# Grouped-query attention on one Trainium2 core: who inverts the softmax row sums, and a new order of the trunk

## The chip, the cores and the metric

The kernel runs on one core of one Trainium2 chip. Its time is the device time of one execution in microseconds (us), and the figure compared is the median over runs. Five engines work side by side, each through a queue of its own in fixed order: TensorE (PE; its weight loads are listed as PEld), VectorE (DVE), ScalarE (ACT), GpSimd (POOL), and SyncE (SP), which issues the DMAs. An engine waits only where its program holds a wait on a semaphore.

## The reference

One encoder layer for two sequences of 1024 and 512 tokens, model width 1024, all float32. Every projection is computed with operands split into a high and a low part. The part that the change touches is the attention of the first block, and there the grouped-query heads:

```python
def _gqa_attention(q, k, v):
    scale = HEAD_DIM ** -0.5
    kf = k.astype(jnp.float32)

    def block(qb):
        s = jnp.einsum('bkgqd,bksd->bkgqs', qb.astype(jnp.float32), kf) * scale
        p = jax.nn.softmax(s, axis=-1)
        return jnp.einsum('bkgqs,bksd->bkgqd', p.astype(v.dtype), v)
...
x = x + jnp.einsum('bse,ed->bsd', jnp.concatenate([d_out, g_out], axis=-1), w_out)
```

d_out comes from four differential heads (two softmaxes, one subtracted from the other), g_out from eight grouped-query heads of width 64 in two groups. Behind the block follow cross-attention to 256 memory tokens, a feed-forward layer with a convolution of width 3, and the last norm.

## The kernel before

The trunk (`trunk_phase`) computes the input projection and all attention of the first block; the rest of the layer is a second program behind it. The trunk goes through six units: 0 to 3 are the differential heads, 4 and 5 the two grouped-query groups. While unit u's attention runs, the projection of unit u + 1 runs between it, 12 tiles of 128 tokens (index i = 12 u + t, so tiles 60 to 71 are unit 5's). Unit 5's attention has no projection beside it.

Attention is cut into 72 pairs. A pair is two tiles of 128 queries of one head against all keys of their sequence. Pairs 24 to 47 are unit 4's, 48 to 71 unit 5's; within a unit four heads of four pairs with 1024 keys come first (the long part), then four heads of two pairs with 512 keys (the short part). A grouped-query pair has two rows of scores (n, one for each query tile) and goes like this:

- PE `score`, DVE `max` (L1153, the negated row maximum), ACT `exp` (L1017, which sums the row as well, into `row_sum`),
- DVE `inverse` (L1158), the reciprocal of the row sum,
- POOL `scale` (L758), which multiplies the row by it in `prob`,
- PE `turn` (L896, four transposes of 128x128 for each 256 keys; the first one waits for both rows' `scale`), ACT `hi` (L1026), DVE `lo` (L1173), PE `mix` (L917), and at the end ACT `out` (L1043), DVE `merge` (L1192), SP `store`.

A tile of a grouped-query projection goes PE `proj` (L843), ACT `nat`, then POOL `v_split` (L698, L702), DVE `head_mean`, POOL `head_rstd` (L707), DVE `head_norm`, POOL `rope`, `turn_round` and `rope_add` (L731 to L752), PE `qk_turn` (L856), ACT `qk_hi`, DVE `qk_lo`. POOL also scales and splits the next unit's weights (`w_scale`, `w_split`: L672, L674) and, in unit 5, splits w_out in 16 steps (`out_split`: L681, L684). `rstd` (L657) is a power of one column.

The order on each engine isn't written by hand. `plan` puts every step with an engine, a due time, a duration and what it comes after; `Plan.placed` then fills the engines in turn. A step's rank is its due time plus a shift out of the table `SHIFT`, by stage (`dl`, `ds`: differential, long and short; `gl`, `gs`: grouped-query; `d`, `g`: projections) and by kind; `PATIENCE` says how long an engine's place is kept for an earlier step. The result is a fixed list of steps for each engine, and the semaphores alone decide when each runs.

## Time and profile before

| what | us |
|---|---|
| median of 3 runs | 2415.27 |
| lowest and highest | 2414.86, 2416.46 |
| the profiled execution | 2416.07 |
| its span, first to last instruction | 2414.3 |
| PE busy | 2356.2 (98%) |
| DVE busy | 1693.5 (70%) |
| POOL busy | 1399.2 (58%) |
| ACT busy | 1016.3 (42%) |

Busy shares are averages over stages that differ. The trunk ends at about 872 us; the rest belongs to the second program. In a row of a timeline the first number is the start in us from the span's start, the second the time to the end of the group, and a bracket at the end tells how long the engine had been idle and who ended that. Matmuls overlap one another, so a busy PE isn't a PE at its peak, and a short wait can hide in a matmul that only looks long.

### The profile page before, as it was taken

The numbers are of one execution on the slowest core, as the hardware profiler recorded it, in microseconds if no ns is written. First come the engines' busy times: TensorE is split into PE (matmuls) and PEld (weight loads), VectorE is DVE, ScalarE is ACT, GpSimd is POOL, SyncE is SP. The second block draws the span as 40 slices with busy tenths as digits, with TensorE's granted clock in tenths as the row PEclk, the third lists the DMA queues.
The fourth block names the chain that finished last, engine by engine and source line by source line (L and its number), as shares of the span: only waits on it lengthen the run. The fifth ranks groups of instructions, "written<-read, shape, count | busy, mean of one in ns | idle before, by whom it ended". The sixth has DMA issues, their size and how long they took to land.

```text
span 2414.3 us, 34261 instructions
## 1 busy us (share of the span) xinstructions
PE 2356.2 (98%) x12306; PEld 2017.4 (84%) x12306; DVE 1693.5 (70%) x2508; ACT 1016.3 (42%) x2047; POOL 1399.2 (58%) x1603
## 2 busy tenths in 40 slices
PE   7999999999999999999999999999999999999997
PEld 6999888888898878888888888888878888888885
DVE  7537777787889963243334388877688888888887
ACT  4436656555668852133332213211243333333334
POOL 5454645689877630053230277767777777777775
PEclk9999999999999999999999999999999999999999
DMA  8743434432212062132244323223321111111112
GB/s 297 248 173 139 158 136 159 159 131 98 96 61 85 13 193 106 45 121 72 100 152 141 138 98 105 92 92 105 140 83 62 53 53 53 53 53 53 53 53 92
DMA packets 102728, 260.40 MB, mean 108 GB/s; under 512 B 10145, under 2 KB 45345, under 8 KB 92065
## 3 DMA queue, kind: packets, MB, share of 16 engines
q1 hardware_dynamic: 101264, 257.82, 31.0%
q8 instruction: 100, 1.64, 0.3%
q14 instruction: 68, 0.55, 0.1%
q10 hardware_dynamic: 1296, 0.39, 0.1%
HBM read 209.95 MB, written 48.23 MB: 107 GB/s over the span
## 4 chain that ended last, share of the span: by engine, by line
PE 57%; DVE 2%; POOL 2%; ACT 1%; issue 1%; DMA 1%; DVEq 0%; POOLq 0%; SPq 0%; ACTq 0%
PE r_bank L2104 27%; PE r_bank L2010 11%; PE r_bank L1981 10%; PE r_bank L2043 5%; PE r_bank L2062 1%; PE r_bank L2091 1%; DVE r_conv L2474 1%; PE r_bank L2025 1%; PE r_bank L2074 0%; DMA r_rows_w<-in_w_up_units 0%; POOL r_s_lo L1849 0%; ACT r_conv L2311 0%; DVE r_x_p L2677 0%; DVE r_x_p L2552 0%; POOL r_w_lo L1849 0%
## 5 line engine op out<-in xcount | busy, mean ns | idle before, releaser
L843 PE MATMUL t_proj<-t_w_hi,t_hbuf 128*128 128x384 f32 x1056 | 311.6, 348 | 2.1 <-ACT t_nat L994 0.9
L2552 DVE TENSOR_TENSOR r_x_p<-r_bank,r_x_p 128x512 f32<-128x512 f32 x320 | 207.9, 683 | 47.1 <-PE r_bank L2104 46.5
L2474 DVE SCALAR_TENSOR_TENSOR r_conv<-r_rows,r_taps,r_conv 128x511 f32<-128x511 f32 (+3 forms) x134 | 182.5, 1362 | 49.4 <-ACT r_conv L2311 47.0
L1153 DVE TENSOR_REDUCE t_max_neg<-t_scores 128x1 f32<-128x1024 f32 (+1 forms) x192 | 196.9, 1038 | 23.8 <-PE t_scores L877 17.8
L1017 ACT ACTIVATE t_prob<-t_scores,t_max_neg 128x1024 f32<-128x1024 f32 (+1 forms) x192 | 187.4, 977 | 48.6 <-DVE t_max_neg L1153 44.5
L843 PEld LDWEIGHTS t_proj<-t_w_hi,t_hbuf 128*128 128x128 f32 x1056 | 194.9, 189 | 8.3 <-issue 6.4
L1026 ACT CAST t_pt_hi<-t_turn 128x512 fp32r<-128x512 f32 x240 | 140.3, 587 | 107.3 <-PE t_turn L896 82.2
L1173 DVE TENSOR_TENSOR t_pt_lo<-t_turn,t_pt_hi 128x512 fp32r<-128x512 f32 x240 | 163.4, 686 | 30.1 <-ACT t_pt_hi L1026 26.4
L843 PE MATMUL t_proj<-t_w_lo,t_hbuf 128*128 128x384 f32 x528 | 177.9, 337 | 0.0
L1776 POOL TENSOR_TENSOR r_stat<-r_stat,minus_half 128x1 f32<-128x1 f32 x24 | 14.1, 589 | 275.7 <-DVE r_stat L2437 275.7
L1831 POOL TENSOR_TENSOR r_w_lo<-r_stage,r_w_hi 128x1024 fp32r<-128x1024 f32 (+1 forms) x86 | 166.3, 1934 | 7.2
L896 PE MATMUL t_turn<-ident,t_prob 128*128 128x128 f32 x960 | 142.6, 274 | 6.2 <-DVE t_pt_lo L1173 4.2
L2278 ACT CAST r_s_hi<-r_s_raw 128x512 fp32r<-128x512 f32 x86 | 53.4, 620 | 219.8 <-POOL r_s_raw L1884 81.5
L917 PE MATMUL t_acc<-t_pt_hi,t_v_hi 128*128 128x256 f32 x480 | 139.0, 307 | 2.2 <-DVE t_pt_lo L1173 1.1
L1828 POOL TENSOR_SCALAR r_w_hi<-r_stage 128x1024 fp32r<-128x1024 f32 (+1 forms) x86 | 85.0, 988 | 93.5 <-PE r_bank L2104 48.7
L1981 PE MATMUL r_bank<-r_hs_hi,r_w_hi 128*128 128x512 f32 x352 | 137.1, 390 | 0.0
L1981 PE MATMUL r_bank<-r_hs_lo,r_w_hi 128*128 128x512 f32 x352 | 137.0, 389 | 0.0
L1981 PE MATMUL r_bank<-r_hs_hi,r_w_lo 128*128 128x512 f32 x352 | 136.9, 389 | 0.0
L2486 DVE TENSOR_TENSOR r_x_s<-r_bank,r_x_s 128x512 f32<-128x512 f32 x176 | 120.3, 688 | 23.0 <-PE r_bank L2104 21.3
L1849 POOL TENSOR_TENSOR r_s_lo<-r_s_raw,r_s_hi 128x512 fp32r<-128x512 f32 x86 | 115.5, 1343 | 35.1 <-ACT r_s_hi L2278 35.1
L2104 PE MATMUL r_bank<-r_wd_hi,r_g_hi 128*128 128x512 f32 x336 | 131.1, 390 | 1.9 <-DVE r_g_lo L2547 1.4
L896 PEld LDWEIGHTS t_turn<-ident,t_prob 128*128 128x128 f32 x960 | 111.8, 140 | 24.3 <-issue 11.6
(307 smaller groups left out, 7282.9 us busy)
## 6 DMA issues: line engine op xcount, KB each, us to landing
t_hbuf<-split_x SPq DMA_DIRECT2D x60, 1024.0 KB, 4.8
r_stage<-in_w_up_units SPq DMA_DIRECT2D x44, 512.0 KB, 3.3
r_rows_w<-in_w_up_units SPq DMA_DIRECT2D x88, 256.0 KB, 3.1
split_x<-t_hbuf SPq DMA_DIRECT2D x12, 1024.0 KB, 5.2
r_stage<-in_w_down SPq DMA_DIRECT2D x22, 512.0 KB, 3.3
r_wd_raw<-in_w_down SPq DMA_DIRECT2D x42, 256.0 KB, 2.7
...
```

The source lines that it names most:

```text
L843: ins = nc.tensor.matmul(proj_bank(i), l, r[:, k, :], start=(k == 0 and j == 0), stop=(k == KT - 1 and j == 2))
L896: ins = nc.tensor.transpose(ps_t[:, slot, kk * 2 * P + qt * P:kk * 2 * P + (qt + 1) * P], prob[:, n % PSLOTS, keys], ident[:, :])
L1017: nc.scalar.activation(prob[:, n % PSLOTS, 0:p.keys], ps_s[:, n % 2, 0:p.keys], ACT.Exp, bias=max_neg[:, n % COLS:n % COLS + 1], accum_out ...
L1026: nc.scalar.copy(pt_hi[:, n % 2, :], ps_t[:, slot, :]).then_inc(pthi_done, 1)
L1153: nc.vector.tensor_reduce(max_neg[:, n % COLS:n % COLS + 1], ps_s[:, n % 2, 0:p.keys], AX.X, ALU.max, negate=True).then_inc(max_done, 1)
L1173: nc.vector.tensor_tensor(pt_lo[:, n % 2, :], ps_t[:, slot, :], f32(pt_hi[:, n % 2, :]), ALU.subtract).then_inc(ptlo_done, 1)
L1831: nc.gpsimd.tensor_tensor(lo, raw, f32(hi), ALU.subtract).then_inc(w_split[s], 1)
L1981: ins = nc.tensor.matmul(one_bank(s), l, r, start=(k == 0 and j == 0), stop=(k == KT - 1 and j == 2))
L2010: ins = nc.tensor.matmul(acc(t)[:, cols], l[:, k, :], r[:, cols], start=(k == 0 and j == 0), stop=(k == KT - 1 and j == 2))
L2104: ins = nc.tensor.matmul(out, l, r, start=(first and j == 0), stop=(last and j == 2), skip_group_check=onto)
L2474: return nc.vector.scalar_tensor_tensor(out, src, tap_of(j, s, i), out, ALU.mult, ALU.add)
L2552: nc.vector.tensor_tensor(x_p[:, t, cols], down_bank(n), x_p[:, t, cols], ALU.add).then_inc(p_add, 1)
```

## The change

The DVE `inverse` of the grouped-query pairs is gone (96 reciprocals; the differential pairs keep their 48). POOL waits for `exp` itself, raises the row sum to the power -1 against a column of -1.0, waits for its own result, and scales as before. In the plan the two steps become one of POOL with 0.55 more time. A rope of a differential tile now waits for the rope before it. `SHIFT` and `PATIENCE` have new values, so that steps of every stage stand in other places.

```diff
-PATIENCE = {"PE": 0.03, "DVE": 0.23, "ACT": 0.36, "POOL": 0.23, "SP": 0.0}
+PATIENCE = {"PE": 0.03, "DVE": 0.26, "ACT": 0.34, "POOL": 0.19, "SP": 0.0}
 SHIFT = {
...
-    "gl": {"exp": -5.7, "hi": -3.5, "inverse": -0.7, "lo": -21.9, "max": -3.2, "merge": -28.7, "mix": 1, "out": -2.2, "scale": 0.3,
+    "gl": {"exp": 3.8, "hi": -3, "inverse": -0.7, "lo": -20.7, "max": -1.3, "merge": -26.7, "mix": 1.4, "out": -2.5, "scale": 0.6,
...
-                put("DVE", b + 3.8 * s, 0.17, "inverse", (p, n), ("exp", (p, n, 0)))
-                put("POOL", b + 4.1 * s, by_seg(1.13, 0.71), "scale", (p, n), ("inverse", (p, n)))
+                put("POOL", b + 3.8 * s, by_seg(1.68, 1.26), "scale", (p, n), ("exp", (p, n, 0)))
...
+            nc.gpsimd.memset(minus_one[:, :], -1.0).then_inc(minus_made, 1)
...
                     if UNITS[u][0] == "diff":
                         pool.wait_ge(nat_filled, i + 1)
+                        if i:
+                            pool.wait_ge(roped, i)
...
                 elif kind == "scale":
                     p, n = what
-                    pool.wait_ge(inv_done, n - 2 * n_diff + 1)
+                    pool.wait_ge(exp_done, n + 1)
+                    if n == 4 * n_diff:
+                        pool.wait_ge(minus_made, 1)
+                    nc.gpsimd.tensor_tensor(inv[:, n % COLS:n % COLS + 1], row_sum[:, n % COLS:n % COLS + 1], minus_one[:, 0:1],
+                                            ALU.pow).then_inc(row_inverted, 1)
+                    pool.wait_ge(row_inverted, n - 4 * n_diff + 1)
```

What the new order looks like at three places follows, of the kernel before and of the changed one. Line numbers of the changed kernel are higher by 1 to 8: L762 is the new power, L766 the scaling, L682 and L685 the two instructions of a split of w_out.

POOL in the long part of unit 5, before, from the scalings of pair 52 to those of pair 53 (`wo_hi`, `wo_lo` are the parts of w_out):

```order
L758 TENSOR_SCALAR t_prob<-t_prob,t_inv 128x1024 x2
L681 TENSOR_SCALAR wo_hi_73<-wo_raw_89 128x512
L684 TENSOR_TENSOR wo_lo_81<-wo_raw_89,wo_hi_73 128x512
L681 TENSOR_SCALAR wo_hi_73<-wo_raw_89 128x512
L684 TENSOR_TENSOR wo_lo_81<-wo_raw_89,wo_hi_73 128x512
L758 TENSOR_SCALAR t_prob<-t_prob,t_inv 128x1024 x2
```

and in the changed kernel, from the second row of pair 52:

```order
L762 TENSOR_TENSOR t_inv<-t_row_sum,t_minus_one 128x1
L766 TENSOR_SCALAR t_prob<-t_prob,t_inv 128x1024
L682 TENSOR_SCALAR wo_hi_73<-wo_raw_89 128x512
L685 TENSOR_TENSOR wo_lo_81<-wo_raw_89,wo_hi_73 128x512
L762 TENSOR_TENSOR t_inv<-t_row_sum,t_minus_one 128x1
L766 TENSOR_SCALAR t_prob<-t_prob,t_inv 128x1024
L682 TENSOR_SCALAR wo_hi_73<-wo_raw_89 128x512
L685 TENSOR_TENSOR wo_lo_81<-wo_raw_89,wo_hi_73 128x512
L762 TENSOR_TENSOR t_inv<-t_row_sum,t_minus_one 128x1
```

Two splits between two pairs have become, mostly, one split between two rows, and they reach on to pair 61 instead of pair 57; each scaling has its power in front.

POOL at the end of unit 4, before, the last tile (71) and pairs 45 to 50 (L731, L739, L744, L750, L752 are its rope):

```order
L707 TENSOR_TENSOR t_vrstd<-t_vstat,minus_half 128x5
L758 TENSOR_SCALAR t_prob<-t_prob,t_inv 128x512 x2
L731 TENSOR_TENSOR t_nat<-t_nat,t_head_gain 128x320
L739 TENSOR_TENSOR t_rot_a<-t_nat,t_cos_g 128x320
L744 TENSOR_TENSOR t_rot_b<-t_nat,t_sin_g 128x5x16 x4
L758 TENSOR_SCALAR t_prob<-t_prob,t_inv 128x512 x2
L750 TENSOR_TENSOR t_nat<-t_rot_a,t_rot_b 128x256
L752 TENSOR_TENSOR t_nat<-t_rot_a,t_rot_b 128x128
L758 TENSOR_SCALAR t_prob<-t_prob,t_inv 128x512
L758 TENSOR_SCALAR t_prob<-t_prob,t_inv 128x1024 x5
```

and in the changed kernel, from the same rope on:

```order
L734 TENSOR_TENSOR t_nat<-t_nat,t_head_gain 128x320
L762 TENSOR_TENSOR t_inv<-t_row_sum,t_minus_one 128x1
L766 TENSOR_SCALAR t_prob<-t_prob,t_inv 128x512
L742 TENSOR_TENSOR t_rot_a<-t_nat,t_cos_g 128x320
L747 TENSOR_TENSOR t_rot_b<-t_nat,t_sin_g 128x5x16 x4
L753 TENSOR_TENSOR t_nat<-t_rot_a,t_rot_b 128x256
L755 TENSOR_TENSOR t_nat<-t_rot_a,t_rot_b 128x128
L762 TENSOR_TENSOR t_inv<-t_row_sum,t_minus_one 128x1
L766 TENSOR_SCALAR t_prob<-t_prob,t_inv 128x512
L762 TENSOR_TENSOR t_inv<-t_row_sum,t_minus_one 128x1
L766 TENSOR_SCALAR t_prob<-t_prob,t_inv 128x1024
```

Pair 47's first scaling has moved ahead of the long turn of tile 71's rope; its second still stands behind the rope's end.

PE at the same place, before: the first transposes of pair 47 (L896), the eight matmuls of pair 46's mix (L917), then tile 71's qk_turn (L856) and the scores of pair 49's second row:

```order
L896 MATMUL t_turn<-ident,t_prob 128x128 x4
L917 MATMUL t_acc<-t_pt_hi,t_v_hi 128x256
...
L917 MATMUL t_acc<-t_pt_lo,t_v_hi 128x256
L856 MATMUL t_turn<-ident,t_nat 128x128 x3
L882 MATMUL t_scores<-t_qk_109 128x512
```

and in the changed kernel:

```order
L864 MATMUL t_turn<-ident,t_nat 128x128 x3
L925 MATMUL t_acc<-t_pt_hi,t_v_hi 128x256
...
L925 MATMUL t_acc<-t_pt_lo,t_v_hi 128x256
L904 MATMUL t_turn<-ident,t_prob 128x128 x4
L890 MATMUL t_scores<-t_qk_109 128x512
```

Tile 71's qk_turn and pair 47's first transposes have changed places around the mix of pair 46.

## Rows read from the trace of the kernel before

**Rows 1.** Busy time by stretch: window, length, then each engine's busy time (instructions).
```profile
150.00:573.00 423.00, 416.91 (x2574) 370.83 (x2573) 310.36 (x587) 242.72 (x635) 260.29 (x552) 1.00 0.42 149
583.10:748.50 165.40, 161.13 (x1083) 148.95 (x1083) 144.73 (x282) 117.33 (x255) 133.76 (x208) 1.00 0.20 68
756.00:837.00 81.00, 80.70 (x579) 73.41 (x578) 78.50 (x136) 71.61 (x133) 64.53 (x64) 1.00 0.22 65
837.00:872.00 35.00, 29.91 (x202) 24.37 (x201) 29.13 (x61) 27.70 (x62) 9.70 (x14) 1.00 0.20 50
```
The engines stand in the order PE, PEld, DVE, ACT, POOL; behind them the granted clock, the DMA share and GB/s.

**Rows 2.** Timeline of DVE in unit 5: start, duration, engine, line, operation.
```profile
814.69 0.15 DVE L1158 RECIPROCAL t_inv<-t_row_sum 128x1 f32<-128x1 f32 x1
814.76 1.21 DVE L1153 TENSOR_REDUCE t_max_neg<-t_scores 128x1 f32<-128x1024 f32 x1
```

**Rows 3.** Line L758: POOL's idle time before it; who waited for it (us, times).
```profile
  DVE t_inv L1158: 49.4, 35
...
  PEld t_turn L896: 4.8, 9
```

**Rows 4.** Timeline of PE: the first transposes of pairs 58, 59 and 62.
```profile
811.82 0.60 PE L896 MATMUL t_turn<-ident,t_prob 128*128 128x128 f32 x4
...
817.32 0.38 PE L896 MATMUL t_turn<-ident,t_prob 128*128 128x128 f32 x2
...
833.55 0.60 PE L896 MATMUL t_turn<-ident,t_prob 128*128 128x128 f32 x4
```

**Rows 5.** Timeline of POOL at the start: a power of one column and its reader.
```profile
31.78 0.56 POOL L657 TENSOR_TENSOR t_rstd<-t_mean_sq,minus_half 128x1 f32<-128x1 f32 x1
32.44 1.19 POOL L661 TENSOR_SCALAR t_mem_diag<-ident,t_rstd 128x128 f32<-128x128 f32 x1
```

**Rows 6.** Timeline of POOL: the scalings of pairs 58 and 59 in one go.
```profile
809.33 4.43 POOL L758 TENSOR_SCALAR t_prob<-t_prob,t_inv 128x1024 f32<-128x1024 f32 x4
```

**Rows 7.** Timeline of POOL: the starts of two splits of w_out that follow each other.
```profile
761.22 0.63 POOL L681 TENSOR_SCALAR wo_hi<-wo_raw 128x512 fp32r<-128x512 f32 x1
...
763.19 0.62 POOL L681 TENSOR_SCALAR wo_hi<-wo_raw 128x512 fp32r<-128x512 f32 x1
```

**Rows 8.** Timeline of ACT: the end of pair 50's first exp, its row sum read out.
```profile
758.23 0.20 ACT L1017 ACTIVATION_READ_ACCUMULATOR t_prob<-t_scores,t_max_neg 128x1 f32 x1
```

**Rows 9.** Timeline of POOL: unit 4's first scalings and its last one.
```profile
583.08 2.25 POOL L758 TENSOR_SCALAR t_prob<-t_prob,t_inv 128x1024 f32<-128x1024 f32 x2
...
747.75 0.69 POOL L758 TENSOR_SCALAR t_prob<-t_prob,t_inv 128x512 f32<-128x512 f32 x1 [0.32 <-DVE t_inv L1158]
```

**Rows 10.** POOL's waits from 583 to 748 us: total, times, longest.
```profile
POOL t_prob L758 <- DVE t_inv L1158: 11.7, 10, 2.8
POOL t_nat L731 <- DVE t_nat L1128: 6.8, 8, 1.6
POOL t_v_hi L698 <- ACT t_nat L994: 5.7, 3, 3.0
POOL t_vrstd L707 <- DVE t_vstat L1122: 4.2, 10, 1.1
```

**Rows 11.** Timeline of POOL: scalings of pairs 48 to 50, first and last of five.
```profile
750.49 1.13 POOL L758 TENSOR_SCALAR t_prob<-t_prob,t_inv 128x1024 f32<-128x1024 f32 x1 [2.05 <-DVE t_inv L1158]
...
760.13 1.13 POOL L758 TENSOR_SCALAR t_prob<-t_prob,t_inv 128x1024 f32<-128x1024 f32 x1 [0.66 <-DVE t_inv L1158]
```

**Rows 12.** Timeline of PE: the first transposes of pair 47.
```profile
749.60 0.60 PE L896 MATMUL t_turn<-ident,t_prob 128*128 128x128 f32 x4
```

**Rows 13.** PE's waits from 500 to 872 us on VectorE's lo: total, times, longest.
```profile
PE t_turn L896 <- DVE t_pt_lo L1173: 4.2, 5, 1.3
...
PE t_acc L917 <- DVE t_pt_lo L1173: 1.1, 2, 0.6
```

**Rows 14.** Timeline of POOL and of PE: pair 38's scalings, then its first transposes.
```profile
693.30 2.40 POOL L758 TENSOR_SCALAR t_prob<-t_prob,t_inv 128x1024 f32<-128x1024 f32 x2 [0.50 <-DVE t_inv L1158]
...
707.81 0.60 PE L896 MATMUL t_turn<-ident,t_prob 128*128 128x128 f32 x4
```

More of the change, by code:

```diff
@@ L131 @@
 RING = {"turn": "lo", "qk_turn": "qk_lo", "sumsq": "sub_mean", "spread": "finish", "total": "mean"}
-PATIENCE = {"PE": 0.03, "DVE": 0.23, "ACT": 0.36, "POOL": 0.23, "SP": 0.0}
+PATIENCE = {"PE": 0.03, "DVE": 0.26, "ACT": 0.34, "POOL": 0.19, "SP": 0.0}
 SHIFT = {
-    "dl": {"coef": -20.2, "combine": 6, "eps_r": 29.7, "exp": 3.9, "finish": 8.6, "hi": 7.7, "inverse": -50.1, "lo": 9, "max":
-          19.8, "mix": 5.2, "out": 11.2, "score": 1.3, "spread": -12.7, "store": 5.4, "sub_mean": 2, "sub_rstd": 11, "sumsq":
-          -72.3, "turn": -0.5},
-    "ds": {"coef": -18.7, "combine": -16.4, "eps_r": -16.7, "exp": -3.3, "finish": -31.2, "hi": -6.7, "inverse": 43.7, "lo": 8.4,
-          "max": -15.7, "mix": 5.1, "out": 7.2, "score": -5.6, "spread": -0.8, "store": 0.8, "sub_mean": 21.1, "sub_rstd": -38.7,
-          "sumsq": -22.8, "turn": 1.8},
-    "gl": {"exp": -5.7, "hi": -3.5, "inverse": -0.7, "lo": -21.9, "max": -3.2, "merge": -28.7, "mix": 1, "out": -2.2, "scale": 0.3,
-          "score": -1.7, "store": 28.5, "turn": 0.4},
-    "gs": {"exp": -4.8, "hi": -4, "inverse": -1.6, "lo": -1.4, "max": -4.5, "merge": -0.6, "mix": -36.7, "out": -2.9, "scale":
-          -0.6, "score": -0.2, "store": -13.7, "turn": 2.5},
-    "g": {"head_mean": -7.2, "head_norm": -8.8, "head_rstd": 16.7, "nat": -2.6, "proj": 0.1, "qk_hi": -42.5, "qk_lo": 15.5,
-         "qk_turn": 0.2, "rope_add": 1.6, "rope": 8, "turn_round": -15.5, "v_split": 16.5},
-    "d": {"nat": -42.3, "proj": -2.8, "qk_hi": 47.1, "qk_lo": 19.3, "qk_turn": 0.2, "rope": 5.3, "v_split": 9.7},
@@ new lines @@
+    "dl": {"coef": -41.7, "combine": 4.1, "eps_r": 25.8, "exp": 6.9, "finish": 18.6, "hi": 15.6, "inverse": -36.8, "lo": 6, "max":
+          9.7, "mix": 6.8, "out": 10.9, "score": 1.3, "spread": 1.6, "store": -22.4, "sub_mean": -28.3, "sub_rstd": -1.1, "sumsq":
+          -76.3, "turn": -0.6},
+    "ds": {"coef": -20.1, "combine": -9.2, "eps_r": -31.7, "exp": 5.7, "finish": -24.6, "hi": -4.7, "inverse": 71.7, "lo": -0.1,
+          "max": -19.8, "mix": 1.8, "out": 6, "score": -4.7, "spread": 0.9, "store": 1.6, "sub_mean": 41.4, "sub_rstd": -60.2,
+          "sumsq": -35.5, "turn": 1.8},
@@ new lines @@
+    "gl": {"exp": 3.8, "hi": -3, "inverse": -0.7, "lo": -20.7, "max": -1.3, "merge": -26.7, "mix": 1.4, "out": -2.5, "scale": 0.6,
+          "score": -1.2, "store": 50.5, "turn": 0.7},
+    "gs": {"exp": -4.5, "hi": -3.6, "inverse": -1.6, "lo": -1.8, "max": -3.6, "merge": -0.3, "mix": -41.4, "out": -3.2, "scale":
+          -9.9, "score": -0.2, "store": 10.9, "turn": 0.7},
+    "g": {"head_mean": -5.4, "head_norm": -11.3, "head_rstd": 17.2, "nat": -1.3, "proj": 0.5, "qk_hi": -37.2, "qk_lo": 20.9,
+         "qk_turn": 0.2, "rope_add": -20.7, "rope": 1.5, "turn_round": 4.7, "v_split": 16.5},
@@ L149 @@
+    "d": {"nat": -34.5, "proj": -2.8, "qk_hi": 53.3, "qk_lo": 10.2, "qk_turn": 0.7, "rope": 7, "v_split": 9.5},
 }
```

3 lines of the change are left out of this document (2 added, 1 removed).

## The prediction

> **What bounds the kernel now.** I read the busy table by stretch first. TensorE (PE) is busy 416.9 of 423.0 us in the differential units, 161.1 of 165.4 in the first grouped-query unit (unit 4, whose pairs are 24 to 47), 80.7 of 81.0 in the long part of unit 5 and 29.9 of 35.0 in its short part and drain [rows 1]. So PE sets the pace, and all that a better order can take back in the trunk is its idle time: 6.1 + 4.3 + 0.3 + 5.1 us, about 16. From 872 us on nothing is changed. In the same rows GpSimd (POOL) is at 133.8 of 165.4 in unit 4 and at 64.5 of 81.0 in unit 5; VectorE (DVE) is at 144.7 and 78.5. The question is whether Pool can take 96 more instructions before it overtakes PE.
>
> **The reciprocal that goes.** One lasts 0.15 us, but on VectorE's queue the next instruction starts 0.07 us after it (814.69 to 814.76) [rows 2]: 96 x 0.07 = 6.7 us of VectorE's time, up to 96 x 0.15 = 14.4 if none overlapped. Its wait also goes: Pool stood 49.4 us before its scalings for VectorE's inverse, which had queued behind lo and max steps [rows 3]. In the steady part of unit 5, pair 58 opens its transposes at 811.82 and pair 59 at 817.32, a period of 5.50 us [rows 4]; PE has no gap in it, so a lighter VectorE gives nothing there. I cost the removal at nothing. PE covers it; what would make it count is rival A.
>
> **The power that comes.** The kernel has a power of one column on Pool already, for rstd, and it is followed once, as the new one always is, by a wait of Pool on itself. It starts at 31.78, lasts 0.56, and the instruction that reads its result starts at 32.44 [rows 5]: 0.66 us from start to start. The bounds are 0.55, if the wait were free, and 0.66. I take 0.655, since every dependent pair on Pool shows the gap. A long scaling takes 1.10 (four in 4.43 us) [rows 6], so a long row now costs Pool 1.755 us. The whole addition is 96 x 0.655 = 63 us of Pool.
>
> **Unit 5: Pool against PE.** Between the scalings Pool splits w_out, 16 times 1.97 us (761.22 to 763.19) [rows 7]. Before, Pool did two splits and two scalings per pair, 6.15 us against PE's 5.50, for eight pairs, and used up its lead: pair 58's scalings began at 809.33, two of them end near 811.5, and its transposes opened at 811.82 [rows 4, 6]. The new order spreads the splits (first order piece). Sum from pair 50, whose first exp is read out at 758.43 [rows 8]: up to the scaling of pair 62 there are 26 rows x 1.755 = 45.6, plus 16 x 1.97 = 31.5, together 77.1, hence 835.6. PE opened pair 62's transposes at 833.55 [rows 4]. So Pool is 2.1 us late there even if it starts pair 50 on time. With 0.55 for the power it would be 74.4 and on time.
>
> **Unit 4: does Pool start pair 50 on time?** From its first scaling at 583.08 to the end of its last at 748.44 Pool has 165.4 us [rows 9]. Its waits for others in that stretch are 11.7 + 6.8 + 5.7 + 4.2 = 28.4 [rows 10], so its own chain takes 137.0. Add 48 x 0.655 = 31.4: 168.4, already 3 us more than there is, with no wait left. Some waits can't go: head_rstd is made on Pool, head_norm on VectorE, rope on Pool again. These were 6.8 us over 8 waits, 0.85 each [rows 10]. In the new order four of the fourteen tiles (58 to 71) still have rope right behind head_rstd, and three have only the short v_split between: 4 x 0.85 and some 0.2 for each of the three, together 4.0. So the last scaling of pair 47 ends near 755.5. Four scalings of pairs 48 and 49 (7.0) bring pair 50 to 762.5, 4.0 us later than its exp allows. Before, Pool had slack here: it waited 2.05 + 0.98 + 1.90 + 1.59 + 0.66 = 7.2 us before the five scalings from 750.49 to 760.13 (the first and the last of the five in [rows 11]), and this is what the new work eats. The lower end is 168.4 with no wait, which brings pair 50 back to 758.5 and the lateness to 2.1 alone. The upper end keeps all 11.0 us of waits on the head chain, which adds 7 more.
>
> In this stretch qk_turn and the first transposes of pair 47 change places on PE, and the last scaling of pair 47 stands behind rope_add on Pool (second and third order piece). PE opened pair 47 at 749.60, 1.16 us behind the scaling [rows 9, 12]. This is where I expect the first PE wait. Queued behind it are the scores of pair 49 and everything later.
>
> **The new order elsewhere.** The table moves steps in every unit. In the differential units Pool's work is unchanged but for a wait of each rope on the one before it, which has long ended; PE's idle time is 6.1 us in 423 [rows 1]. A new order could win or lose some 2 us of this; I take zero. SP's stores move by a place or two; the out_loads now stand ahead of pair 47's store, which delays nothing that is short. The drain at the end keeps its order: most of PE's waits for VectorE's lo are there, the longest 1.3 us [rows 13], and reciprocals stood ahead of it. There, and in the rest of unit 5's short part (5.1 us idle), I take 1 us back, since VectorE catches up while PE is late.
>
> **Sum.** 2.1 (unit 5) + 4.0 (unit 4) - 1 (drain) = +5.1, taken as +5. The profiled execution took 2416.07 with a span of 2414.3, so 1.8 us lie around the span; the median of the three runs is 2415.27, 0.8 below it. On the profiled one that gives 2421.1, against the median 2420.3.
>
> **A rule against this.** VectorE is the busiest of the three elementwise engines in unit 5, 97% against Pool's 80% [rows 1]. The Trainium skill, Perfetto Trace Analysis, Identifying the Most-Contended Engine, says that for Vector, Scalar and GPSIMD the occupancy tells how close an engine is to its limit, and to optimize the busiest engine first. By that rule the change moves load the right way, and the sum would be rival A's, not mine. The rows speak against it as far as they go: an average of 80% hides that Pool runs without a pause for eight pairs.
>
> **Rivals.**
> A. VectorE is the real pace-setter beside PE, and the change is faster. Mechanism: lo steps come 0.07 to 0.15 us earlier and never sit behind an inverse that waits for exp, so PE's waits on them go. From 500 to 872 us those are 4.2 + 1.1 = 5.3 us [rows 13]; nearly all of it, with a little of the rest of PE's idle time, is 5.5, giving 2409.8. It decides if Pool's lead never falls to zero. Against it: nine weight loads of transposes waited 4.8 us for Pool [rows 3], so Pool had little to give already. Chance 0.15.
> B. Pool's lag stays inside its lead. In the middle of unit 4 that is long: pair 38's second scaling ends at 695.70 and its transposes open at 707.81 [rows 14]. The new order also puts most of unit 4's qk_turn steps later. If Pool's waits vanish and scalings are ordered well, only small changes are left: -1.5 us, 2413.8, within 2 us either way. Chance 0.27.
> C. Pool holds PE up as summed: 2420.3, from +1 to +11. Chance 0.45. This is the forecast.
> D. The order of the differential units turns out worse: exp, combine and lo change places there too, and if a transpose comes to wait in each of the 24 pairs for 0.25 us, PE's idle time of 6.1 us [rows 1] doubles: 2421.3. Nothing in the profile speaks for it but the many moved steps. Chance 0.13.
>
> **How the numbers follow.** About 0.2%, 4.8 us, is what a measurement of this kernel can tell from no change. C straddles that bound: two thirds of it above (0.30), one third within (0.15). B is within but for 0.05. A is faster but for 0.03. D is slower but for 0.03. That makes faster 0.14, same 0.43, slower 0.43. The range leaves out A's better half and C's and D's worst ends: 2410.5 to 2427.
>
> **What would show it.** If C holds, Pool has hardly any idle time from 583 to 830 us, and the list of PE's waits has transposes waiting for t_prob from Pool, the first near pair 47 and qk_turn 71, again between pairs 53 and 62. The power followed by the scaling shows 0.65 us from start to start, and the span from 583 to 837 us grows while 872 to the end stays at 1542. If A holds, that stretch shrinks and VectorE shows gaps. If B holds, Pool is near 98% busy in unit 4 and PE doesn't wait for it. If D holds, the stretch up to 573 us grows. I am wrong at the root if the power costs under 0.5 us, or if the splits of w_out are far shorter than 1.97 between two powers.

## The result and the profile after

The changed kernel takes 2421.84 us (median of 10 runs, 2419.12 to 2424.03) against 2415.61 for the kernel before (10 runs, 2414.86 to 2416.46): a ratio of 1.0024, 95% interval 1.0016 to 1.0033, 6.2 us slower. The forecast was 2420.3, slower by 5. The number was nearly right. The profile shows another cause than the one that made it. The profiled execution of the changed kernel took 2424.03 with a span of 2421.9, so it is the longest of the ten.

First the stretches, as in [rows 1] (window, length, busy time of PE, PEld, DVE, ACT and POOL with instructions, granted clock, DMA share, GB/s):

```profile
150.00:573.00 423.00, 416.84 (x2575) 370.73 (x2574) 309.89 (x589) 242.73 (x632) 259.64 (x555) 1.00 0.42 150
583.00:749.00 166.00, 162.37 (x1094) 150.10 (x1093) 141.19 (x241) 118.92 (x258) 154.97 (x251) 1.00 0.20 68
756.00:837.00 81.00, 76.52 (x531) 70.31 (x530) 71.10 (x93) 66.18 (x122) 73.47 (x85) 0.96 0.20 64
```

Up to 573 us the busy times are those of before. In unit 4 POOL is up by some 21 us and PE is as busy as before. In the long part of unit 5 PE is at 76.52 of 81.0 where it had 80.70, and the granted clock is 0.96: the loss is there. PE's waits from 583 to 837 us (who waited for what: us in total, times, longest):

```profile
PE t_acc L925 <- DVE t_mixed L1200: 4.4, 1, 4.4
...
PE t_turn L904 <- POOL t_prob L766: 0.6, 1, 0.6
...
```

All but the first lie in unit 4 and at its end and come to 4.3 us; before, PE's waits in the same 254 us were 4.9, of which 0.9 for POOL. POOL, the engine of the forecast, costs PE one wait of 0.6 us (pair 48). The large one is a wait of `mix` (L925) for VectorE's merge, and the merge had waited for a DMA. The timelines of DVE and then of PE there (start, duration, and in brackets the idle time before with its releaser):

```profile
774.87 0.42 DVE L1200 TENSOR_TENSOR t_mixed<-t_acc,t_sq 64x256 f32<-64x256 f32 x1 [4.76 <-DMA mix_scratch<-t_mixed]
```

```profile
775.43 0.55 PE L925 MATMUL t_acc<-t_pt_hi,t_v_hi 128*128 128x256 f32 x1 [4.40 <-DVE t_mixed L1200]
776.00 0.41 PE L925 MATMUL t_acc<-t_pt_hi,t_v_hi 128*128 128x256 f32 x1
...
777.28 1.05 PE L904 MATMUL t_turn<-ident,t_prob 128*128 128x128 f32 x4
...
781.84 0.60 PE L904 MATMUL t_turn<-ident,t_prob 128*128 128x128 f32 x4
```

DVE stood 4.76 us before the merge of pair 49, which writes the same half of `mixed` as pair 47 and must wait until pair 47's store has landed. PE stood 4.40 us before the mix of pair 50, which waits for that merge. After the wait a matmul of the mix lasts 0.41 us and four transposes 1.05, until at 781.84 four transposes take their usual 0.60 again. In the windows around it the granted clock is the last but two number:

```profile
770.00:775.00 5.00, 1.03 (x7) 0.66 (x5) 0.24 (x2) 1.50 (x3) 4.71 (x7) 0.93 0.73 229
775.00:780.00 5.00, 4.57 (x17) 4.21 (x18) 3.40 (x5) 2.21 (x4) 4.47 (x5) 0.50 0.06 15
780.00:785.00 5.00, 5.00 (x38) 4.78 (x36) 4.03 (x5) 3.32 (x7) 4.11 (x6) 0.88 0.06 13
```

PE hardly ran until 775, and came back with a clock of 0.50, the lower of its two levels (1.2 of 2.4 GHz), from 775 to 780.

SP's queue shows why the store was late. After, and then before (`x8` is a group of eight; the second number is the time to the group's end):

```profile
756.91 13.89 SPq L633 DMA_DIRECT2D wo_raw<-in_w_out  x8
770.84 29.34 SPq L624 DMA_DIRECT2D mix_scratch<-t_mixed  x7
```

```profile
756.34 3.99 SPq L633 DMA_DIRECT2D wo_raw<-in_w_out  x3
760.38 0.45 SPq L624 DMA_DIRECT2D mix_scratch<-t_mixed  x1
761.29 9.62 SPq L633 DMA_DIRECT2D wo_raw<-in_w_out  x5
```

The store of pair 47 is the single one at 760.38 before. In the changed kernel it is the first of the seven at 770.84, behind all eight out_loads of 512 KB each, which SP issues some 1.74 us apart. It lands 4.0 us after its issue, while the loads are moving 229 GB/s; the store behind it takes 3.7, and those issued once the loads have ended take 1.9. Before, the same store took 4.4 us, also among loads, so it is late by its issue, 770.84 in place of 760.38, and not by its transfer. The Trainium skill, DMA: Bandwidth & Descriptors, Latency and other measured facts, says that a DMA's fixed cost grows with the load on HBM, which is where this store goes; the 4.0 against 1.9 us fits that, but would fit as well a store that only queues behind the loads' data, and no run here tells the two apart.

How late each pair is shows where time goes. The table has the opening of a pair's transposes against the kernel before, with the lateness at pair 0 taken off (it varies from -0.8 to +0.9 us between executions), from each kernel's profiled execution. "Minus before" is median against the median of before on the same chip.

| kernel | median us | minus before | at pair 50 | pair 50 to 62 | pair 62 to 71 |
|---|---|---|---|---|---|
| changed kernel | 2421.84 | +6.2 | +0.3 | +7.0 | 0.0 |
| x1 changed, store ahead of out_load 3 | 2417.62 | +1.4 | +0.2 | +1.9 | 0.0 |
| x2 before, store behind out_load 7 | 2423.99 | +7.7 | +0.7 | +7.5 | 0.0 |
| x3 power, order of before | 2434.75 | +18.5 | +8.9 | +9.7 | 0.0 |
| x4 new order, reciprocals, no power | 2425.11 | +8.8 | +6.2 | +0.1 | +3.1 |
| x5 changed, store behind out_load 5 | 2417.33 | +0.9 | -0.2 | +1.8 | 0.0 |
| x6 changed, store behind out_load 6 | 2420.09 | +3.6 | -0.3 | +4.8 | 0.0 |
| x7 as x1, reciprocals as well | 2421.46 | +5.0 | +1.9 | +1.7 | +3.3 |
| x8 as x3, reciprocals as well | 2432.39 | +15.9 | +7.9 | +9.5 | 0.0 |
| x9 as x1, splits spread | 2416.58 | +0.2 | +0.1 | +0.3 | 0.0 |
| x10 before with the new table, store ahead | 2424.10 | +7.7 | +7.6 | -0.1 | +0.5 |
| x11 as x3, splits spread | 2425.51 | +9.1 | +8.9 | +4.1 | 0.0 |
| x12 as x9, drain moved | 2415.32 | -1.7 | +0.1 | +0.8 | -1.8 |

### The profile page after: what moved, and what is told of

Its sections match the earlier page's. It is cut to its first block, busy times and chain, and to the rows that moved or that the text cites. A ratio compares the mean times of both kernels' runs of the same rounds, so it can differ in the third digit from the quotient of the medians.

```text
span 2421.9 us, 34310 instructions
## 1 busy us (share of the span) xinstructions
PE 2358.8 (97%) x12306; PEld 2019.2 (83%) x12306; DVE 1683.4 (70%) x2412; ACT 1016.8 (42%) x2047; POOL 1447.2 (60%) x1700
## 4 chain that ended last, share of the span: by engine, by line
PE 57%; DVE 2%; POOL 2%; ACT 1%; issue 1%; DMA 1%; DVEq 0%; POOLq 0%; SPq 0%; ACTq 0%
PE r_bank L2112 27%; PE r_bank L2018 11%; PE r_bank L1989 10%; PE r_bank L2051 5%; PE r_bank L2070 1%; PE r_bank L2099 1%; DVE r_conv L2482 1%; PE r_bank L2033 1%; PE r_bank L2082 0%; DMA r_rows_w<-in_w_up_units 0%; POOL r_s_lo L1857 0%; ACT r_conv L2319 0%; DVE r_x_p L2685 0%; DVE r_x_p L2560 0%; POOL r_w_lo L1857 0%
## 5 line engine op out<-in xcount | busy, mean ns | idle before, releaser
L1839 POOL TENSOR_TENSOR r_w_lo<-r_stage,r_w_hi 128x1024 fp32r<-128x1024 f32 (+1 forms) x86 | 166.3, 1934 | 7.2
L925 PE MATMUL t_acc<-t_pt_hi,t_v_hi 128*128 128x256 f32 x480 | 139.8, 308 | 7.4 <-DVE t_mixed L1200 5.4
```

Of the source, the lines that this page charges most:

```text
L1839: nc.gpsimd.tensor_tensor(lo, raw, f32(hi), ALU.subtract).then_inc(w_split[s], 1)
```

## The store

The first theory: all of the loss is the store's place on SP. The rival: Pool is late as forecast, and the stall only hides it.

**x1, the store back in its old place.**

```diff
     order = plan(pairs, bounds)
+    sp = order["SP"]
+    late = next(s for s in sp if s[1] == "store" and s[2][0].no == 47)
+    sp.remove(late)
+    sp.insert(next(z for z, s in enumerate(sp) if s[1:] == ("out_load", (3,))) + 0, late)
```

> The changed kernel, with one step of SyncE's queue moved: the store of pair 47 stands ahead of out_load 3, where the kernel before has it, in place of behind out_load 7. Nothing on any other engine moves. The theory of the store: in the changed kernel pair 51 opens its transposes 7.7 us later than before, and from there the lateness stays at 7.6 to 7.7 to the end of the trunk; all of it is the 4.8 us that VectorE waited for this store's transfer, passed on to TensorE (4.4), and what TensorE lost after it. So this kernel loses all of that: pair 51 within 1 us of the kernel before, 2414 to 2416 us, 6 to 8 below the changed kernel. The theory of the prediction, Pool as the bound: with the stall gone Pool's lateness comes out, TensorE waits for t_prob at pairs 53 to 62, 2.1 us by the prediction's sum for unit 5, so 2417 to 2418; with its whole sum of 5, 2420.

Measured: 2417.62 (2416.90 to 2418.79), 1.0005 of before (0.9996 to 1.0014). Of the 6.2 us above before 1.4 are left. The jump of 7.0 between pairs 50 and 51 is gone; pairs 51 and 50 are both 0.25 us earlier than before. But the time is not back at before's: 1.9 us are lost between pairs 50 and 62. PE's waits from 755 to 837 us in this kernel:

```profile
PE t_turn L908 <- POOL t_prob L770: 1.8, 2, 1.4
```

These are pair 53 (0.37) and pair 58 (1.39), and there is no other wait in the stretch. So both theories hold in part: the store made the loss of the changed kernel, and behind its stall lay the lateness of Pool, 1.9 us where the prediction's sum has 2.1.

**x2, the same fault put into the kernel before.** Here only the store moves, behind out_load 7.

```diff
     order = plan(pairs, bounds)
+    sp = order["SP"]
+    late = next(s for s in sp if s[1] == "store" and s[2][0].no == 47)
+    sp.remove(late)
+    sp.insert(next(z for z, s in enumerate(sp) if s[1:] == ("out_load", (7,))) + 1, late)
```

> The kernel before (reciprocals on VectorE, its own order), with one step moved: the store of pair 47 stands behind out_load 7, as in the changed kernel, in place of ahead of out_load 3. The theory of the store: the merge of pair 49 waits some 4 to 5 us for the transfer, TensorE's mix of pair 50 waits with it, and what follows is at the low clock for a few us: 6 to 8 us slower than before, 2421 to 2424, with the jump between pairs 50 and 51 and nothing else changed. The rival, that the store only hurts together with Pool's new load (Pool being the bound): within 1 us of before, since Pool here has its old work.

Measured: 2423.99 (2423.24 to 2424.96), 7.7 above before. The wait and its releaser are the same as in the changed kernel:

```profile
775.36 0.55 PE L921 MATMUL t_acc<-t_pt_hi,t_v_hi 128*128 128x256 f32 x1 [5.13 <-DVE t_mixed L1196]
```

One DMA issue of 64 KB, moved on a queue where nothing computes, costs 7.7 us without any change to Pool or VectorE. The rival falls.

**x5 and x6, the store one and two places earlier than the change has it.** The edit is x1's, with `("out_load", (5,))` or `("out_load", (6,))` and `+ 1`.

> The changed kernel with the store of pair 47 behind out_load 5, two places earlier than the change has it. The out_loads are issued some 1.74 us apart (eight from 756.91 to 770.84), so the store lands 3.5 us earlier and TensorE's wait for the mixed tile of pair 50 should be 4.4 - 3.5 = 0.9 us in place of 4.4. In the changed kernel pair 51 is 7.0 us later against pair 50, of which 4.4 are the wait and 2.6 the low clock behind it. If the clock falls after any such wait, the jump is 0.9 + 2.6 = 3.5 and the time near 2421; if a wait this short leaves the clock alone, the jump is 0.9 and the time stays within 1 us of the kernel with the store ahead of out_load 3 (2417.6), since Pool's lateness of 1.9 up to pair 62 hides under those 0.9 partly.

> The changed kernel with the store of pair 47 behind out_load 6, one place earlier than the change has it: the wait should be 4.4 - 1.7 = 2.7 us. If what follows the wait is the low clock at the same price as in the changed kernel, the jump from pair 50 to pair 51 is 2.7 + 2.6 = 5.3 and the time near 2421; if the price grows with the wait, less than 2.6 is added; if the clock stays up, the jump is 2.7 and the time is near 2418.5, Pool's lateness of unit 5 then being hidden behind it.

Measured: 2417.33 (2416.36 to 2419.15) and 2420.09 (2417.95 to 2423.01). The stalls of PE in them, in that order:

```profile
770.22 0.36 PE L929 MATMUL t_acc<-t_pt_hi,t_v_hi 128*128 128x256 f32 x1 [0.25 <-DVE t_mixed L1204]
```

```profile
774.13 0.55 PE L929 MATMUL t_acc<-t_pt_hi,t_v_hi 128*128 128x256 f32 x1 [3.54 <-DVE t_mixed L1204]
```

and the window behind x6's stall:

```profile
775.00:780.00 5.00, 5.00 (x31) 4.76 (x31) 3.46 (x5) 3.11 (x6) 4.72 (x7) 0.76 0.06 15
```

Put together, with the lateness gained from pair 50 to pair 53:

| kernel | PE's wait for `mixed`, us | lateness gained | beyond the wait |
|---|---|---|---|
| x5 | 0.25 | 0.29 | 0.0 |
| x12 | 0.78 | 0.80 | 0.0 |
| x11 | 2.55 | 4.11 | 1.6 |
| x6 | 3.54 | 5.01 | 1.5 |
| changed | 4.40 | 6.97 | 2.6 |
| x2 | 5.13 | 7.52 | 2.4 |

A wait of 0.25 us, or one of 0.78 (x12, which gains 0.80), leaves the clock at 1.00 in every window. Behind one of 3.54 it is 0.76 from 775 to 780, behind one of 4.40 it is 0.50. The price of the clock was 1.5 to 1.6 us in two kernels and 2.4 to 2.6 in two, so of the cases in the two expectations the one of a short wait that leaves the clock alone (x5) and the one of a price that isn't constant (x6) came true. The waits themselves missed: 0.25 for 0.9, and 3.54 for 2.7. SP doesn't issue the out_loads evenly, 1.74 us is only their mean: in the changed kernel out_load 5 goes out at 765.67 and out_load 6 at 768.85. So x5's store went out 5.5 us earlier (765.37) and not 3.5, and x6's 1.6 earlier (769.20), with a landing of 4.3 us in place of 4.0 and a PE that had come to the mix 0.45 us earlier.

## Pool, and the power against the reciprocal

**x3, the power alone.** The changed kernel's code with the table and the planner's lines of before; the `inverse` of a grouped-query pair is skipped on VectorE.

```diff
-PATIENCE = {"PE": 0.03, "DVE": 0.26, "ACT": 0.34, "POOL": 0.19, "SP": 0.0}
+PATIENCE = {"PE": 0.03, "DVE": 0.23, "ACT": 0.36, "POOL": 0.23, "SP": 0.0}
...
-                put("POOL", b + 3.8 * s, by_seg(1.68, 1.26), "scale", (p, n), ("exp", (p, n, 0)))
+                put("DVE", b + 3.8 * s, 0.17, "inverse", (p, n), ("exp", (p, n, 0)))
+                put("POOL", b + 4.1 * s, by_seg(1.13, 0.71), "scale", (p, n), ("inverse", (p, n)))
...
                 elif kind == "inverse":
                     p, n = what
+                    if not p.diff:
+                        continue
```

> The power alone: Pool inverts the row sums, VectorE's reciprocals of the grouped-query units are gone, and all engines keep the order of the kernel before (its table of numbers), the store ahead of out_load 3 included. By the arithmetic of Pool: in the first eight pairs of unit 5 it has two splits of 1.97 and two rows of 1.755 per pair, 7.45 us against TensorE's 5.50, 1.3 us per pair more than before, where its lead was just used up by pair 58; so some 10 us late at pair 58, and in unit 4 its own chain of 137.0 + 31.4 us against 165.4 with 11 us of waits on the head chain that the old order has, up to 7 us more. That gives 2425 to 2432, with many waits of TensorE for t_prob. The theory that Pool has room enough in any order: within 1.5 us of before, 2414 to 2417, and then the new order was needed for nothing and only did harm by the store.

Measured: 2434.75 (2434.08 to 2435.36), 18.5 above before, 2.8 more than the upper end of what I expected. Of the 8.9 us up to pair 50, 0.7 are lost in the differential units, at 465 us, where PE waits 1.2 us for a `lo` in place of 0.4; the only step that is new there is the wait of each rope on the one before it, and no run here takes that apart. Five pairs in a row, 54 to 58, each lose another 1.9 us. PE's waits in the long part of unit 5, and Pool's timeline over one pair:

```profile
PE t_turn L905 <- POOL t_prob L767: 9.7, 8, 1.7
```

```profile
797.97 0.55 POOL L763 TENSOR_TENSOR t_inv<-t_row_sum,t_minus_one 128x1 f32<-128x1 f32 x1
798.63 1.13 POOL L767 TENSOR_SCALAR t_prob<-t_prob,t_inv 128x1024 f32<-128x1024 f32 x1
799.72 0.55 POOL L763 TENSOR_TENSOR t_inv<-t_row_sum,t_minus_one 128x1 f32<-128x1 f32 x1
...
801.46 0.62 POOL L683 TENSOR_SCALAR wo_hi<-wo_raw 128x512 fp32r<-128x512 f32 x1
802.16 1.29 POOL L686 TENSOR_TENSOR wo_lo<-wo_raw,wo_hi 128x512 fp32r<-128x512 f32 x1
...
805.38 0.55 POOL L763 TENSOR_TENSOR t_inv<-t_row_sum,t_minus_one 128x1 f32<-128x1 f32 x1
```

From 797.97 to 805.38 Pool does two powers, two scalings and two splits without a pause, 7.41 us; PE's pair takes 5.50. The prediction's arithmetic gives 2 x 1.755 + 2 x 1.97 = 7.45. The power starts 0.66 us ahead of the scaling, and the scaling 1.09 ahead of the next step.

**x11, the power with the splits alone placed anew.** x3 with these lines; x9 is x1 with them.

```diff
+    pool = order["POOL"]
+    splits = [s for s in pool if s[1] == "out_split"]
+    pool[:] = [s for s in pool if s[1] != "out_split"]
+    for k, s in enumerate(splits):
+        pool.insert(next(z for z, x in enumerate(pool) if x[1] == "scale" and x[2][1] == pairs[50 + k].score + 1) + 1, s)
```

> The power in the order of before (2434.75), and of the new order only one thing: the 16 splits of w_out spread to one behind the second scaling of each pair from 50 to 65. In the run without that, pair 58 opened 9.6 us later against pair 53 than before, 1.9 us in each of five pairs, which is Pool's 7.45 us per pair against 5.50. By the same arithmetic with one split (5.48 against 5.50) nothing of it is left: 2425. The 8.9 us lost up to pair 50 stay, since unit 4 is as it was. If it falls by much less, the loss of unit 5 was not the splits.

Measured: 2425.51 (2423.82 to 2429.11), the 2425 of the expectation. From pair 53 to pair 62 nothing is lost any more, where x3 lost 9.6. The profiled execution is the slowest of the five: a merge in it waited 2.90 us for the store of pair 48, which took 6.3 us to land, so the late stores are still there. The 8.9 us up to pair 50 stay, as expected.

**x9, the changed kernel with the store ahead and the splits spread.** (The changed kernel has its 16 splits at pairs 50 to 61, most pairs with one; "two per pair" in the expectation is wrong.)

> The changed kernel with the store of pair 47 ahead of out_load 3 (2417.6), and Pool's 16 splits of w_out placed anew: one behind the second scaling of each pair from 50 to 65, in place of two per pair from 50 to 61. By Pool's arithmetic a pair then costs it 2 x 1.755 + 1.97 = 5.48 us, TensorE's period is 5.50, and what is left falls to pairs 63 to 65, where the scalings had 2 to 5 us to spare. In the kernel with the store ahead, pair 62 is 1.9 us later against pair 50 than before, with waits of 0.37 and 1.39 for t_prob. If Pool's splits make that, it goes: 2415.7. If another engine is late behind it (VectorE's lo, ScalarE's exp), the waits change their name and the time stays within 0.5 us of 2417.6.

Measured: 2416.58 (2415.63 to 2418.73), 1.0001 of before (0.9992 to 1.0010). The loss from pair 50 to 62 falls from 1.9 to 0.3, and PE's list for the long part of unit 5 has one row left:

```profile
PE t_acc L934 <- DVE t_mixed L1209: 0.2, 1, 0.2
```

So the change has two faults of order, one hidden behind the other, and with both mended it is as fast as the kernel before, not faster.

**Is the reciprocal worth nothing on VectorE?** Two kernels keep the power and put the 96 reciprocals back beside it, into a tile that nobody reads: x7 on x1's order, x8 on x3's. x4 is x7 without the power, its scaling waiting for the reciprocal as before.

```diff
+    dve = order["DVE"]
+    for p in pairs:
+        if p.diff:
+            continue
+        for n in (p.score, p.score + 1):
+            step = (0.0, "inverse", (p, n))
+            at = next((z for z, s in enumerate(dve) if s[1] == "max" and s[2][1] == n + 2), None)
+            if at is None:
+                at = next(z for z, s in enumerate(dve) if s[1:] == ("lo", (pairs[69], n - 190)))
+            at = min(at, next(z for z, s in enumerate(dve) if s[1] == "max" and s[2][1] == n) + 6)
+            dve.insert(at, step)
```

> The new order alone: the changed kernel's order on every engine, with the store of pair 47 ahead of out_load 3 as in the experiment above, but the reciprocals back on VectorE (each about two steps of max behind its own row), Pool without the power. Beside the kernel with the store ahead, this is the power against the reciprocal and nothing else. If Pool is the bound in it: 2 to 5 us faster than that one. If neither Pool nor VectorE sets the pace: within 1 us of it. If VectorE's lightened queue is what the change is worth (rival A): up to 5.3 us slower than it, the waits of TensorE for lo growing by as much.

> The kernel with the store ahead of out_load 3 (changed order, power on Pool, 2417.6), with VectorE's 96 reciprocals put back beside it, at the places that they had in the run of the order alone (2425.1); their result goes to a tile that nobody reads. So power and reciprocals both run. Rival A, that the reciprocals' place in VectorE's queue costs TensorE time in this order: the whole 7.5 us between those two runs are theirs, and this kernel is at 2424 to 2426. The theory of the prediction, that VectorE has room and the removal is worth nothing: within 1 us of 2417.6, and the 7.5 us of the run of the order alone came from Pool's scalings starting later, behind an inverse that VectorE makes late. In that run TensorE's waits between 640 and 740 us were for t_qk (1.8), t_pt_lo (1.7) and t_mixed (1.1), all written by VectorE, which speaks for the former.

> The run of the power in the order of before (2434.75), with VectorE's 96 reciprocals also left where the kernel before has them, their result going to a tile that nobody reads. Power and reciprocals both run; the difference to that run is what the removal alone gave in the old order, the difference to before is what the power alone costs. The prediction costed the removal at nothing: within 1 us of 2434.75. Rival A: slower than that by up to 5.3 us. VectorE is freed of 6.7 to 14.4 us, so if all of it told, it would be 2441 to 2449.

Measured: x4 2425.11 (2424.95 to 2426.27), x7 2421.46 (2420.55 to 2424.13), x8 2432.39 (2432.27 to 2434.05).

| | reciprocals only | both | power only |
|---|---|---|---|
| order of before | 2416.3 (before) | 2432.4 (x8) | 2434.8 (x3) |
| new order, store ahead | 2425.1 (x4) | 2421.5 (x7) | 2417.6 (x1) |

In the old order the removal of the reciprocals gains nothing; with them the kernel is even 2.4 us faster. 1.2 of that is in the trunk, the rest before pair 0, and I have no cause for it. In the new order x1 is 3.8 us faster than x7, and x7 3.6 faster than x4. What each difference is made of shows in the traces. First x7 against x1, whose profiled executions are 4.9 us apart at pair 71 (the medians 3.8). By the table of lateness 1.7 us arise up to pair 50 and 3.3 behind pair 62. The 3.3 begin at one place, DVE's and then PE's timeline in x7:

```profile
843.66 0.17 DVE L1182 RECIPROCAL t_spare<-t_row_sum 128x1 f32<-128x1 f32 x1 [1.96 <-ACT t_prob L1040]
843.74 1.27 DVE L1197 TENSOR_TENSOR t_pt_lo<-t_turn,t_pt_hi 128x512 fp32r<-128x512 f32 x2
```

```profile
844.47 0.38 PE L940 MATMUL t_acc<-t_pt_hi,t_v_hi 128*128 128x256 f32 x1 [2.14 <-DVE t_pt_lo L1197]
```

My rule put the reciprocal of pair 65's first row ahead of the last two lo of pair 62. It waited 1.96 us for exp, the two lo stood behind it, PE stood 2.14 us, and the granted clock from 845 to 850 was 0.66. x4 has the same place and loses 3.1 there. The planner's own places (x10, below) have that reciprocal behind the two lo, and the loss is 0.5. So the larger part of the difference is a place of my own choosing, and what the reciprocals cost in this order otherwise is the 1.7 us up to pair 50 or a little less. No run moves that one step alone.

Then x4 against x7, which have the same list of steps on every engine and differ in Pool's scaling: in x7 it has the power ahead of it and waits for exp, in x4 it waits for VectorE's reciprocal. From 583 to 756 us, in x4:

```profile
POOL t_prob L776 <- DVE t_inv L1176: 27.3, 21, 3.9
```

In x7 it never does. x4 is 6.2 us late at pair 50, x7 1.9. PE's waits for VectorE from 640 to 740 us, in x4,

```profile
PE t_turn L914 <- DVE t_qk L1166: 1.8, 1, 1.8
PE t_turn L874 <- DVE t_pt_lo L1191: 1.5, 1, 1.5
PE t_acc L935 <- DVE t_mixed L1210: 1.1, 1, 1.1
PE t_acc L935 <- DVE t_pt_lo L1191: 0.2, 1, 0.2
```

and in x7:

```profile
PE t_acc L940 <- DVE t_mixed L1216: 1.1, 1, 1.1
...
PE t_turn L879 <- DVE t_pt_lo L1197: 0.3, 1, 0.3
PE t_acc L940 <- DVE t_pt_lo L1197: 0.2, 1, 0.2
```

They come to 4.6 and 1.6 us; in x1 it is 0.5. VectorE's name stands on all of x4's, but 3.0 of the 4.6 go with the same reciprocals still on VectorE, as soon as Pool no longer waits for them. Whether other places for the reciprocals would save the loss up to pair 50 is what x10 tests.

**x10, the new table alone,** in the kernel before, with x1's store.

> The kernel before with nothing but the changed table of numbers, the reciprocals on VectorE and put in their places by the planner itself (a median of seven steps behind their row's max, like before), and the store of pair 47 ahead of out_load 3. In the run of the order alone the reciprocals stood at places of my own choosing, one to six steps behind the max. If their places made the loss there (2425.1), this kernel is well below it, 2416 to 2418. If the new numbers need a VectorE without reciprocals, it stays at 2421 or more, with TensorE's waits for t_qk, t_pt_lo and t_mixed between 640 and 740 us.

Measured: 2424.10 (2423.28 to 2425.29), 1.0 us below x4. The planner's own places take away the loss behind pair 62 (0.5 for 3.1) but not the one up to pair 50 (7.6). So the new numbers need the reciprocals off VectorE's path to Pool. By x4 against x7 (6.2 and 1.9 us at pair 50) Pool's wait for them is the larger part of that and their time on VectorE the smaller; for the planner's own places no run takes the two apart. Each half of the change alone costs time (18.5 and 7.7 us); together, with the store mended, they cost 1.4. The comparison is of the tables, not of one order, since 237 of the 1113 places in PE's list hold another step when the planner has reciprocals to place.

**x12, the drain.** In nearly all these kernels PE waits for VectorE's lo at pairs 70 and 71. In x9, DVE and then PE there:

```profile
861.67 1.22 DVE L1214 TENSOR_TENSOR h_lo<-h_raw,h_hi 128x1024 fp32r<-128x1024 f32 x1
862.80 0.69 DVE L1190 TENSOR_TENSOR t_pt_lo<-t_turn,t_pt_hi 128x512 fp32r<-128x512 f32 x1
```

```profile
863.64 0.63 PE L913 MATMUL t_turn<-ident,t_prob 128*128 128x128 f32 x4 [1.24 <-DVE t_pt_lo L1190]
...
867.21 0.63 PE L913 MATMUL t_turn<-ident,t_prob 128*128 128x128 f32 x4 [1.05 <-DVE t_pt_lo L1190]
```

A step of 1.22 us (`mix_lo`, L1214) stands right ahead of a lo, and at 865.19 another, of 1.28; in the kernel before, a reciprocal between them took 0.07. x12 moves those two, and the two casts of ACT that they wait for.

```diff
+    act, dve = order["ACT"], order["DVE"]
+    for queue, kind, behind in ((act, "mix_hi", [("hi", (pairs[70], 1)), ("hi", (pairs[71], 1))]),
+                                (dve, "mix_lo", [("lo", (pairs[70], 1)), ("lo", (pairs[71], 1))])):
+        for t, at in enumerate(behind):
+            step = next(s for s in queue if s[1:] == (kind, (t,)))
+            queue.remove(step)
+            queue.insert(next(z for z, s in enumerate(queue) if s[1:] == at) + 1, step)
```

> The kernel with the store ahead and the splits spread (2416.6), and in the drain four steps moved: ScalarE's mix_hi of tiles 0 and 1 behind hi of pair 70 and of pair 71, VectorE's mix_lo of the same tiles behind lo of pair 70 and of pair 71. In that kernel, and in every other one here, TensorE waits 1.24 and 1.04 us for lo at pairs 70 and 71. The prediction said that reciprocals stood ahead of those lo steps and took 1 us back with them; without reciprocals the waits are the same. Theory: it is the mix_lo steps of 1.22 and 1.28 us, which stand right ahead of lo on VectorE. Moved, the waits go, up to the 1.8 us that Pool's scaling of pair 71 has to spare, less some 0.3 at the end where mix_lo now delays the last merge: 2415.1, 1.5 below that kernel and 1.3 below the kernel before. If the lo steps are late for another reason (hi, exp), the waits stay and so does the time.

Measured: 2415.32 (2414.16 to 2417.16), 0.9995 of before (0.9986 to 1.0004), so not told apart from it. PE's timeline:

```profile
864.14 0.63 PE L920 MATMUL t_turn<-ident,t_prob 128*128 128x128 f32 x4 [0.41 <-DVE t_pt_lo L1197]
...
870.84 0.36 PE L941 MATMUL t_acc<-t_pt_hi,t_v_hi 128*128 128x256 f32 x1 [1.31 <-DVE t_mixed L1216]
...
874.41 0.76 PE L2034 MATMUL r_bank<-wo_hi,h_hi 128*128 128x512 f32 x1 [2.32 <-PEq L454]
```

The wait at pair 70 falls from 1.24 to 0.41 and the one at pair 71 is gone; pair 71 opens 1.8 us earlier against pair 62. But the last mix now waits 1.31 us for a merge that stands behind a moved `mix_lo`, and the second program's first matmul comes at 874.41. From the opening of pair 62 to that matmul it is 39.35 us, against 40.13 in x9: 0.8 us gained. (Counted from pair 0 only 0.26 is left of it, since this execution lost 0.5 us more at pair 51, whose mix waited 0.78 us for a merge in place of 0.21.) The medians of x12 and x9 are 1.3 us apart, from two chips and with intervals that overlap, so they don't tell 0.8 from the 1.5 that I expected. The cause was right; by the traces about half of the gain came, since the wait moved on by one pair.

## The prediction, step by step

- **The power, 0.655 us from its start to the scaling's.** Right: 0.64 to 0.67 us in 90 of the 96 cases, at most 1.25. A long row costs 1.73 to 1.75 (forecast 1.755). From there:

```profile
750.08 0.70 POOL L766 TENSOR_SCALAR t_prob<-t_prob,t_inv 128x512 f32<-128x512 f32 x1
750.74 0.55 POOL L762 TENSOR_TENSOR t_inv<-t_row_sum,t_minus_one 128x1 f32<-128x1 f32 x1
751.39 1.12 POOL L766 TENSOR_SCALAR t_prob<-t_prob,t_inv 128x1024 f32<-128x1024 f32 x1
752.48 0.55 POOL L762 TENSOR_TENSOR t_inv<-t_row_sum,t_minus_one 128x1 f32<-128x1 f32 x1
...
759.41 0.55 POOL L762 TENSOR_TENSOR t_inv<-t_row_sum,t_minus_one 128x1 f32<-128x1 f32 x1 [0.33 <-ACT t_prob L1025]
```

- **The splits, 1.97 us.** Right: 761.16 to 763.13 in the changed kernel.
- **Unit 5, +2.1 us.** Right as a mechanism and nearly in size, but not what the changed kernel paid. x1 shows it bare: +1.9, with waits at pairs 53 and 58, and x9 takes it away. In the changed kernel PE stood still for 4.40 us and Pool caught up: from pair 52 to 65 its scalings end 3 us or more ahead of the transposes.
- **Unit 4, +4.0 us.** Wrong: +0.2 at pair 50 in x1. Pool's last scaling of pair 47 starts at 750.08 and ends at 750.78, where the sum put its end near 755.5. The 4.7 us are three terms. The chain began at 581.4 in place of 583.08, since the new order has the splits of the next weights elsewhere, which before kept Pool from 579.90 to 583.08 (1.7). Its waits were 3.1 in place of 4.0 (0.9). And its own work came to 166.3 in place of 168.4 (2.1), which isn't one kind of step. The groups of Pool's `v_split` in unit 4, before and then after:

```profile
L698 POOL TENSOR_SCALAR t_v_hi<-t_nat 128x64 fp32r<-128x64 f32 x14 | 5.5, 391 | 5.7 <-ACT t_nat L994 5.7
L702 POOL TENSOR_TENSOR t_v_hi<-t_nat,t_v_hi 128x64 fp32r<-128x64 f32 x14 | 4.6, 331 | 1.2
```

```profile
L703 POOL TENSOR_TENSOR t_v_hi<-t_nat,t_v_hi 128x64 fp32r<-128x64 f32 x14 | 6.0, 431 | 1.2
L699 POOL TENSOR_SCALAR t_v_hi<-t_nat 128x64 fp32r<-128x64 f32 x14 | 3.4, 244 | 0.0
```

  The copy takes 14 x (391 - 244) ns = 2.1 us less, but the subtraction behind it 14 x (431 - 331) = 1.4 us more, and the 16 short scalings take 16 x (737 - 697) = 0.6 less; with the long ones (0.3 less) these four groups give 1.6 us; the rest is spread over the others and the gaps. The prediction took before's durations as fixed. The Trainium skill, GPSIMD Engine Reference, Key points, says that Pool shares its SBUF interfaces with VectorE and is in contention with VectorE's instructions that have two SBUF inputs or run in a 2-port mode; that would fit steps that change their time with their place in the order, one way or the other, but no run here tests it. One reading of the new order was off as well: three tiles (66, 67, 69) have rope right behind head_rstd, not four. Pool then waits 1.32 and 0.33 us for exp at pairs 49 and 50, so rival B's mechanism, a lag inside the lead, is what happened in unit 4. The first wait for Pool came at pair 48 (0.64) rather than 47.
- **The drain, -1 us.** Wrong: 0.0. The reciprocals ahead of lo were not what made it late (x12).
- **SP's stores, nothing.** This is the step that failed: "the out_loads now stand ahead of pair 47's store, which delays nothing that is short." It delayed the merge of pair 49 by 4.76 us and the mix of pair 50 by 4.40, and 2.6 us more were lost at the lower clock behind it. The prediction had the order of SP before it and stopped at the transfer itself. It did not ask who reuses the store's source buffer, and what was issued ahead of it: five more out_loads than before (the "place or two" is five), which put its issue 10.5 us later.
- **The differential units, nothing.** Right: at pair 24 the changed kernel is 0.2 us later against pair 0 than before. Rival D falls.
- **The removal, nothing.** Right against the order of before (x8). Inside the new one x7 puts it at 3.8 us (4.9 in the profiled executions), but 3.3 of the 4.9 begin at one reciprocal that I put at a bad place; the 1.7 up to pair 50 are left. So rival A's mechanism, reciprocals ahead of lo, exists, but it only pays back part of what the new order costs by itself (x10, +7.7). The rule that the prediction quoted against itself, to relieve the busiest elementwise engine first (the Trainium skill, Perfetto Trace Analysis, Identifying the Most-Contended Engine), gives the wrong sign in the old order: there the load put on Pool costs 16 to 18.5 us (x8, x3), because Pool, at 80% on average, had no time left where it counts.
- **The sum.** +5 forecast, +6.2 measured between the medians. It was 2.1 + 4.0 - 1 by the prediction; it is 7.0 for the store, 0.3 for all between pair 0 and pair 50 and 0.0 for the drain in the profiled execution, the longest of the ten. The term of unit 5 stayed hidden behind the store's stall, that of unit 4 did not come, and one that wasn't in the sum made the time: they came out alike by chance. With the store mended (x1, +1.4), a forecast of +5 would have been 3.6 us too high.
